# Modulation sums as column groups inside the value projection, squares of two layer norms added on VectorE

## The reference, cut to what matters

```python
cs = jax.nn.silu(c)
for i in range(2):
    mod = cs @ ada_w[i] + ada_b[i]                 # 1024 -> 3072
    shift, scale, gate = jnp.split(mod, 3, axis=-1)
    h = x * (1.0 + scale) + shift
    y = moba_branch(h, ...) if i == 0 else gdn_branch(h, ...)
    x = layer_norm(ALPHA * x + gate * y, ln_g[i], ln_b[i])
```

## Time and profile before

| | before |
|---|---|
| median of three runs | 837.98 us |
| profiled execution: span from first to last instruction | 836.7 us |
| TensorE matmul busy | 818.6 us, 98% |
| TensorE weight load busy | 764.5 us, 91% |
| VectorE busy | 613.2 us, 73% |
| ScalarE busy | 488.0 us, 58% |
| GpSimd busy | 67.8 us, 8% |
| bytes moved | 153.85 MB, mean 184 GB/s |

### The profile page before, as it was taken

The page is one execution under the profiler, slowest core; times in us unless marked ns, Lnnn a source line. Parts: engine busy times, 40 slices in busy tenths (PEclk is TensorE's granted clock), DMA queues, the critical chain, the costliest instruction groups (busy, mean ns, idle before and its releaser), DMA issues.

```text
span 836.7 us, 17639 instructions
## 1 busy us (share of the span) xinstructions
PE 818.6 (98%) x6596; PEld 764.5 (91%) x6596; DVE 613.2 (73%) x1052; ACT 488.0 (58%) x901; POOL 67.8 (8%) x71
## 2 busy tenths in 40 slices
PE   6999999999999999999999999999999999999997
PEld 3899988999998998989898888999999999999885
DVE  4497876768889666977877779664777996888543
ACT  3444476567699754584665457566556554555444
POOL 1000002400001002224100011000002120000000
PEclk9999999999999999999999999999999999999999
DMA  9999963804452221445543426433445444554521
GB/s 373 389 361 389 362 260 140 348 14 139 172 191 103 102 103 52 157 146 192 212 159 143 152 84 219 152 136 141 178 177 201 167 186 156 196 174 177 201 101 50
DMA packets 22012, 153.85 MB, mean 184 GB/s; under 512 B 2496, under 2 KB 2752, under 8 KB 3904
## 3 DMA queue, kind: packets, MB, share of 16 engines
q1 hardware_dynamic: 20592, 145.69, 47.7%
q0 software_dynamic: 1360, 7.34, 2.4%
HBM read 151.97 MB, written 1.05 MB: 183 GB/s over the span
## 4 chain that ended last, share of the span: by engine, by line
PE 83%; DVE 6%; DMA 5%; ACT 3%; issue 2%; SPq 0%; DVEq 0%; ACTq 0%
PE ps L403 41%; PE ps L1277 7%; PE ps L506 7%; PE ps L476 4%; DVE w_lo L1970 3%; PE ps L437 2%; PE ps L843 2%; DMA raw<-in_mixed 2%; PE ps L446 1%; PE ps L468 1%; ACT w_hi L1317 1%; DMA raw<-in_moba_first 1%; DMA proj<-in_ada_first 1%; PE ps L580 1%; PE ps L603 1%
## 5 line engine op out<-in xcount | busy, mean ns | idle before, releaser
L1970 DVE TENSOR_TENSOR w_lo<-raw,w_hi 128x1024 fp32r<-128x1024 f32 x230 | 285.8, 1247 | 95.6 <-ACT w_hi L1317 94.2
L1317 ACT CAST w_hi<-raw 128x1024 fp32r<-128x1024 f32 (+1 forms) x230 | 239.8, 1050 | 165.1 <-PE ps L403 63.1
L403 PE MATMUL ps<-in_hi,w_hi 128*128 128x256 f32 x1120 | 160.7, 286 | 0.5 <-DVE w_lo L1970 0.5
L403 PE MATMUL ps<-in_lo,w_hi 128*128 128x256 f32 x1120 | 157.2, 283 | 0.0
L403 PE MATMUL ps<-in_hi,w_lo 128*128 128x256 f32 x1120 | 157.1, 283 | 0.0
L403 PEld LDWEIGHTS ps<-in_hi,w_hi 128*128 128x128 f32 x1120 | 144.3, 191 | 4.9 <-issue 3.7
L403 PEld LDWEIGHTS ps<-in_hi,w_lo 128*128 128x128 f32 x1120 | 144.5, 192 | 0.0
L403 PEld LDWEIGHTS ps<-in_lo,w_hi 128*128 128x128 f32 x1120 | 144.3, 192 | 0.0
L2235 DVE SCALAR_TENSOR_TENSOR proj<-work,params,proj 128x256 f32 (+1 forms) x72 | 35.7, 496 | 8.0 <-ACT proj L1537 1.9
L2047 DVE SCALAR_TENSOR_TENSOR work<-raw,cs,work 128x1024 f32 x24 | 30.8, 1284 | 4.8 <-DVE w_lo L1970 1.6
L1277 PE MATMUL ps<-w_hi,in_hi 128*128 128x512 f32 x88 | 34.2, 389 | 0.0
(11 more groups left out here) (444 smaller groups left out, 1350.6 us busy)
## 6 DMA issues: line engine op xcount, KB each, us to landing
raw<-in_mixed SPq DMA_DIRECT2D x24, 1024.0 KB, 7.1
raw<-in_ffn_up SPq DMA_DIRECT2D x22, 1024.0 KB, 4.8
raw<-in_gdn_in SPq DMA_DIRECT2D x16, 1024.0 KB, 4.8
raw<-in_w_in SPq DMA_DIRECT2D x16, 1024.0 KB, 4.8
raw<-in_merge SPq DMA_DIRECT2D x12, 1024.0 KB, 4.7
raw<-in_ffn_down SPq DMA_DIRECT2D x11, 1024.0 KB, 4.8
raw<-in_branch SPq DMA_DIRECT2D x6, 1024.0 KB, 4.7
raw<-in_moba_out SPq DMA_DIRECT2D x4, 1024.0 KB, 7.2
```

Of the source, the lines that this page charges most:

```text
L403: mm = pe.matmul(half(u if bank is None else bank, 0), w[:, u, k * P:(k + 1) * P], a[:, base + k, :], start=(n == 0 and k == 0), stop=(n = ...
L1317: act.copy(w_hi[:, u, :], src).then_inc(hi_done, 1)
L1970: dve.tensor_tensor(w_lo[:, u, :], src, w_hi[:, u, :].bitcast(F32), ALU.subtract).then_inc(lo_done, 1)
```

## The change

Three edits. **First**, `add_partitions` sums all three chunks at once, behind `moba_values(0)` and a wait for all 24 blocks: 12 matmuls, ones as weights of 32 columns, the accumulator streaming in quarters of 256 columns to four groups of 32 output partitions. ScalarE copies the rows out, six transposes between `moba_values(1)` and `moba_values(2)` turn them, and VectorE adds the biases there; ln0 has no modulation left. **Second**, the late products of chunk 5 run in one go before the squares of ln0, one column group per part, are copied by ScalarE and turned by two transposes behind the squares; the matmuls of L819 are gone, and `keep_warm` issues three instead of four. **Third**, in ln0 and ln1 VectorE adds the eight square tiles into one (`add_squares`), and TensorE sums that one; in ln0 one low part moves from ahead of `centre` to behind the additions, in ln1 the sum moves into unit 2 of `mem_kv`, ahead of its last eight matmuls.

```diff
@@ -252,7 +252,8 @@
     late_in = [area(0, PAIR * D, of=kv_flat)] + [area(PAIR * D * n, PAIR * D, of=flat_proj) for n in range(3)]
-    late_rows = vnat_flat
+    late_rows = area(0, S, of=vnat_flat)
+    mod_rows = area(3072, 3 * S)
     gain = area(4096, D)
@@ -281,6 +282,12 @@
         return t.rearrange("p a b -> p (a b)")
+    mod_banks = flat(ps[:, 6:8, :])[:, 0:3 * S]
+    def turned_columns(v):
+        return v.rearrange("p (x q r) -> p q x r", x=2, q=4)[:, :, :, 0]
@@ -393,10 +400,12 @@
     def _(pe):
-        def unit(u, tag=None, base=0, bank=None):
+        def unit(u, tag=None, base=0, bank=None, before_last=None):
             for n, (w, a) in enumerate(((w_hi, in_hi), (w_hi, in_lo), (w_lo, in_hi))):
+                if n == 2 and before_last:
+                    before_last()
                 for k in range(UNIT):
@@ -414,14 +423,12 @@
-        def project_short(name, tag, base=0, between={}, first=0, count=None):
+        def project_short(name, tag, base=0, within={}, first=0, count=None):
                 pe.wait_ge(taken, FIRST[name] + n + 1)
-                unit(n % GROUP, tag if n == 0 else None, base)
-                if n in between:
-                    between[n]()
+                unit(n % GROUP, tag if n == 0 else None, base, before_last=within.get(n))
@@ -491,12 +498,10 @@
-        def sum_tiles(out, src, ready, name, tiles=KT):
-            for k in range(tiles):
-                pe.wait_ge(*after(ready, k + 1))
-                mm = pe.matmul(out, ones, src[:, k, :], start=(k == 0), stop=(k == tiles - 1))
-            mm.then_inc(sem(name), 1)
+        def sum_squares(tag):
+            pe.wait_ge(sem(f"{tag}_added"), 1)
+            pe.matmul(half(5, 0), ones, sq_of[tag][:, 0, :], start=True, stop=True).then_inc(sem(f"{tag}_sumsq"), 1)
@@ -643,13 +648,20 @@
-        def add_partitions(chunks, name):
-            for c in chunks:
-                for n in range(KT):
-                    mm = pe.matmul(ps[:, 7, c * KT + n:c * KT + n + 1], acc[:, c, n * P:(n + 1) * P], ones[:, 0:1],
-                                   start=True, stop=True)
-            mm.then_inc(sem(name), 1)
+        def add_partitions():
+            for c in range(3):
+                for q in range(4):
+                    mm = pe.matmul(half(6 + c // 2, c % 2)[32 * q:32 * q + 32, :], ones[:, 0:32],
+                                   acc[:, c, q * S:(q + 1) * S], start=True, stop=True)
+            mm.then_inc(sem("mod_rows"), 1)
+        def turn_rows():
+            pe.wait_ge(sem("mod_copied"), 1)
+            for n in range(6):
+                mm = pe.transpose(mod_banks[:, n * P:(n + 1) * P], mod_rows[:, n * P:(n + 1) * P], ident)
+            mm.then_inc(sem("mod_columns"), 1)
@@ -723,9 +735,11 @@
         pe.wait_ge(*after("consts_in", 16))
-        pe.wait_ge(lo_done, MIXED + 16)
-        add_partitions(range(0, 1), "mod_gate")
-        for n in range(1, GROUP):
+        pe.wait_ge(lo_done, PLAIN)
+        add_partitions()
+        moba_values(1)
+        turn_rows()
+        for n in range(2, GROUP):
             moba_values(n)
@@ -788,36 +802,22 @@
-        def sum_squares(tag):
-            sum_tiles(half(5, 0), sq_of[tag], f"{tag}_sq", f"{tag}_sumsq")
         sum_total(half(4, 0), "ln0", lambda k: (x_t, (taken, all_taken("moba_out", k + 1))), "ln0_sum")
-        def late_products(p):
-            pe.wait_ge(sem("late_in"), 16 * 4)
-            for k in range(KT):
-                q = 32 * (k % 4)
-                mm = pe.matmul(ps[q:q + 32, (6, 4)[p // 2], (p % 2) * S:(p % 2 + 1) * S], cs_wide[:, k, :],
-                               late_in[p][:, k * S:(k + 1) * S], start=(k < 4), stop=(k >= 4))
-            if p % 2:
-                mm.then_inc(sem("late_products"), 1)
-        late_products(0)
-        late_products(1)
-        add_partitions(range(1, 2), "mod_rest")
+        pe.wait_ge(sem("late_in"), 16 * 4)
+        for k in range(KT):
+            for q in range(4):
+                mm = pe.matmul(half(6, 0)[32 * q:32 * q + 32, :], cs_wide[:, k, :], late_in[q][:, k * S:(k + 1) * S],
+                               start=(k == 0), stop=(k == KT - 1))
+        mm.then_inc(sem("late_products"), 1)
         sum_squares("ln0")
-        add_partitions(range(2, 3), "mod_rest")
-        pe.wait_ge(*after("ln0_centred", KT))
-        late_products(2)
-        late_products(3)
-        keep_warm(4, 3)
+        pe.wait_ge(sem("late_copied"), 1)
+        for x in range(2):
+            mm = pe.transpose(half(7, 0)[:, x * P:(x + 1) * P], late_rows[:, x * P:(x + 1) * P], ident)
+        mm.then_inc(sem("late_columns"), 1)
+        keep_warm(3, 3)
         first_units("gdn_in", "in2")
-        pe.wait_ge(*after("late_copied", 2))
-        for n in range(KT):
-            mm = pe.matmul(ps[:, 5, n:n + 1], late_rows[:, n * P:(n + 1) * P], one, start=True, stop=True)
-        mm.then_inc(sem("late_columns"), 1)
         pe.wait_ge(sem("gate_w_lo"), 2)
@@ -1115,7 +1115,7 @@
         memory_pass(2).then_inc(unit_done, 1)
-        project_short("mem_kv", None, base=MEM_IN, between={1: lambda: sum_squares("ln1")}, first=1, count=4)
+        project_short("mem_kv", None, base=MEM_IN, within={2: lambda: sum_squares("ln1")}, first=1, count=4)
         for n in range(4, 8):
@@ -1504,7 +1504,10 @@
-        for n in range(28, 32):
+        high("moba_in", 28)
+        act.wait_ge(sem("mod_rows"), 1)
+        act.copy(mod_rows, mod_banks).then_inc(sem("mod_copied"), 1)
+        for n in range(29, 32):
             high("moba_in", n)
@@ -1516,6 +1519,8 @@
         squares("ln0", x_t, "ln0_centred")
+        act.wait_ge(sem("late_products"), 1)
+        act.copy(late_rows, half(6, 0)).then_inc(sem("late_copied"), 1)
         root("ln0", LN_EPS)
@@ -1526,10 +1531,6 @@
                 act.copy(in_hi[:, k - 1, :], h_t[:, k - 1, :]).then_inc(sem("in2_hi"), 1)
-        for n, bank in enumerate((6, 4)):
-            act.wait_ge(*after("late_products", n + 1))
-            act.copy(late_rows[:, n * 512:(n + 1) * 512], ps[:, bank, :]).then_inc(sem("late_copied"), 1)
         def evac_conv(i, u):
@@ -2012,14 +2013,6 @@
-        def modulation(at, chunks, column, one_plus=None):
-            link(dve.tensor_tensor(flat_mod[:, KT * at:KT * (at + chunks)], ps[:, 7, column:column + KT * chunks],
-                                   param("ada_b", KT * at, KT * chunks), ALU.add))
-            if one_plus is not None:
-                scale = flat_mod[:, one_plus * KT:one_plus * KT + KT]
-                link(dve.tensor_scalar(scale, scale, 1.0, None, ALU.add))
         pair_of = lambda v: v.rearrange("p (a b) -> p a b", a=2)
@@ -2117,12 +2110,20 @@
-        dve.wait_ge(*after("mod_gate", 1))
-        modulation(2, 1, 0)
+        low("moba_in", 28)
+        dve.wait_ge(sem("mod_columns"), 1)
+        for c in range(2, 5):
+            by_pair = lambda v: v.rearrange("p (q x) -> p q x", q=4)
+            ins = dve.tensor_tensor(by_pair(flat_mod[:, KT * c:KT * c + KT]), turned_columns(mod_banks[:, (c - 2) * S:(c - 1) * S]),
+                                    by_pair(param("ada_b", KT * c, KT)), ALU.add)
+        link(ins)
         dve.sem_inc(sem("mod_read"), 1)
-        for n in range(28, 31):
-            low("moba_in", n)
+        low("moba_in", 29)
+        link(dve.tensor_scalar(mod[:, 1, 8:16], mod[:, 1, 8:16], 1.0, None, ALU.add))
+        link(dve.tensor_tensor(ln_bias[:, 0, :], param("ln_b", 0, KT), mod[:, 1, 8:16], ALU.mult))
+        link(dve.tensor_tensor(ln_bias[:, 0, :], ln_bias[:, 0, :], mod[:, 1, 0:8], ALU.add))
+        link(dve.tensor_scalar(ln_bias[:, 1, :], param("ln_b", 0, KT), ALPHA, None, ALU.mult))
+        low("moba_in", 30)
         dve.wait_ge(*after("consts_in", 16))
@@ -2185,6 +2186,16 @@
+        def add_squares(tag):
+            v = sq_of[tag]
+            dve.wait_ge(*after(f"{tag}_sq", 4))
+            dve.tensor_tensor(v[:, 0:2, :], v[:, 0:2, :], v[:, 2:4, :], ALU.add)
+            dve.wait_ge(*after(f"{tag}_sq", KT))
+            link(dve.tensor_tensor(v[:, 4:6, :], v[:, 4:6, :], v[:, 6:8, :], ALU.add))
+            link(dve.tensor_tensor(v[:, 0:2, :], v[:, 0:2, :], v[:, 4:6, :], ALU.add))
+            dve.tensor_tensor(v[:, 0, :], v[:, 0, :], v[:, 1, :], ALU.add).then_inc(sem(f"{tag}_added"), 1)
         def invert(tag):
@@ -2202,13 +2213,11 @@
             residual("moba_out", n, mod[:, 0, 16 + n:17 + n])
-            low("moba_out", n + GROUP)
+            if n < KT - 1:
+                low("moba_out", n + GROUP)
         centre("ln0")
-        dve.wait_ge(*after("mod_rest", 2))
-        modulation(3, 2, KT, one_plus=4)
-        link(dve.tensor_tensor(ln_bias[:, 0, :], param("ln_b", 0, KT), mod[:, 1, 8:16], ALU.mult))
-        link(dve.tensor_tensor(ln_bias[:, 0, :], ln_bias[:, 0, :], mod[:, 1, 0:8], ALU.add))
-        link(dve.tensor_scalar(ln_bias[:, 1, :], param("ln_b", 0, KT), ALPHA, None, ALU.mult))
+        add_squares("ln0")
+        low("moba_out", KT - 1 + GROUP)
         invert("ln0")
```

(4 more changed lines are left out.)

## The result

The changed kernel takes 841.71 us (median of 7 runs, 837.06 to 844.26), the kernel before on the same chip 838.41 (7 runs). The ratio is 1.0033, 95% interval 1.0019 to 1.0048: slower by 0.33%, 2.8 us; the two medians differ by 3.3. 841.3 was forecast. The median is nearly the forecast's; the trace shows that this isn't because every term was.

The account below looks back on a forecast made before the run. TensorE, almost never idle in a hand-written order, was taken to bound the kernel. Terms: wait +6.8, clock +2.3, ln0 -3.4, columns 0, ln1 -2.4, together +3.3 on 837.98, giving 841.3 us; range 838.4 to 843.6.

Parts of the forecast that it names:

- The added wait, +6.8: Value projection: TensorE idles 6.5 us for the last `ada_w` block, plus sums 1.6, transposes 0.7, less 2.0 removed.
- rival (b): Value projection: last block added x earlier than 107.75, gap shrinks by x, clock holds; faster from x = 2.7; chance 0.09.
- a hole under 4 us: Sign against the prediction: TensorE's hole behind the first value piece, forecast at 6.5 us, measures under 4 us.
- an attention less than 6 us later: Sign against the prediction: the attention starts less than 6 us later than in the kernel before.
- The clock, +2.3: Behind the value projection's hole: TensorE's clock falls to its lower level, costing 2.3 us; bounds nothing and 2.3.
- ln0, -3.4: Layer norm 0: scaling starts 3.0 us earlier, and the shorter hold before the first unit gives 0.4 more.
- Rival (d): Layer norm 0: its gaps bring the clock down there too, another 2.3 us, total 843.6; chance 0.08.
- The columns, 0: Behind gdn_in's first units: 1.84 us of records go, but VectorE's chain ends last, so gain 0; bounds 0 and -1.8.
- Rival (c): Behind gdn_in's first units: the columns' 1.8 us are kept as gain, total 839.5; chance 0.08.
- ln1, -2.4: Layer norm 1: sixteen square-sum records become two, -2.8 us, less 0.2 of waiting and 0.2 lost.
- hangs on ScalarE's squares, which don't move: Step in the ln1 term: GpSimd's running sum for the next norm, ending at 380.25, stays put; 0.2 us lost.
- Rival (a), the clock holds: Value projection: the clock stays up through the gap, so the change costs +1.0, total 839.0; chance 0.15.

Follow-up runs that it names:

- after: The changed kernel itself, in its first profiled execution, the fastest of seven: 837.06 us (median of the seven 841.71 us, ratio 1.0033).
- after_again: The changed kernel, unaltered, run once more for a second profile: 841.51 us, ratio 1.0032 to the kernel before.
- gap_warm: The changed kernel with 8 matmuls on constants, result unread, ahead of TensorE's wait for all blocks: 841.32 us, ratio 1.0033 to the kernel before.
- gap_full: The changed kernel with 13 matmuls on constants in the hole ahead of the sums by column groups: 839.54 us, ratio 1.0015 to the kernel before.
- hole: Kernel before with column-group sums behind the third value piece, ln1 additions, and a TensorE wait for the gate activation before gdn_in's later groups: 840.43 us.
- sums_only: The kernel before with only the first edit (sums by column groups); squares, late products and columns unchanged: 843.29 us, ratio 1.0056.
- filler_late: The changed kernel, sums behind the third value piece, plus four unread matmuls where chunk 5's column products stood: 834.23 us, ratio 0.9956 to the kernel before.

## Why the prediction was right, and where it wasn't

**The added wait, +6.8: right mechanism, wrong as a fixed size.** The hole is there, ended by VectorE's last addition, and nothing behind it gives it back. But 6.5 was read from one execution, and the last block's end differs between executions by 4 us: 104.65 and 106.01 in the changed kernel, 104.81 to 108.69 in the others, 107.75 in before. Before, TensorE doesn't wait for that block and no run shows it; in the four traces with the sums in this place (`after`, `after_again`, `gap_warm`, `gap_full`) the time follows the start of the sums, and the clock where it fell, within 0.5 us. The changed kernel's seven runs spread over 7.2 us, the seven of before beside them over 2.4 (later sets: 3.5 of 7 runs, 4.1 of 24). The prediction took the block's pace for that of the weights arriving. That is half of it: in `after_again` VectorE's last five blocks, each with its low part, follow each other every 2.6 to 2.8 us, with pauses of 0.35 at most, so at the end VectorE's own work sets the pace. What differs stands before: ScalarE's longest wait for a load, at 73 to 79 us, is 3.42 in the fastest execution, 4.55 in `after_again`, 4.84 in before. That the loads make the spread is argued from these waits; no run held them fixed. A last block earlier by x was rival (b), and the fastest execution is it: x = 3.1, the clock held. The forecast gives 841.3 - 2.3 - 3.1 = 835.9 for it and it took 837.06. The execution nearest to the median that has a trace (`after_again`, 841.66) had 5.2. The prediction named a hole under 4 us and an attention less than 6 us later as signs against it: both were so in the fastest execution, neither in the next (5.19; 119.35 is 7.9 later).

**The clock, +2.3: right that it falls, too small.** The median run's mean clock is 0.995, and the fall cost 2.76 in `after_again`, above the 2.3 that the prediction held for the upper bound. It didn't at 3.85 us and did at 4.32, 4.71 and 5.19. The start of the kernel was the right place to look: the granted clock reads 0.50 behind the hole, and 1.00 at the start, where records take twice their time all the same. The Trainium skill ("TensorE: Matmul & The Clock Gate", the section on why this matters) has a gap between bursts bring the clock down. `hole` and `after_again` agree; in the gap of 3.85 us it did not happen.

**ln0, -3.4: right, -3.45, though the additions don't earn it.** The centre, the additions, the root and the hold of `keep_warm` came as written. But `sums_only` has all but 0.1 of it without the additions on VectorE. Two things were late before: the squares' sum, because the sums of chunk 3 stood ahead of it on TensorE, and the scaling, because VectorE waited for the modulation and made five small operations behind it; 1.7 us each, and both leave with the sums. The prediction followed the new chain rightly, centre, additions, root, but it is no gain of the additions: the scaling starts 8.35 us behind the total in the whole change (164.89 to 173.24) and 8.05 without them. Rival (d) is refuted: the two gaps of 1.6 and 1.5 us leave the clock at its upper level.

**The columns, 0: right**, -0.13 by the trace and nothing in `filler_late`. Rival (c) falls.

**ln1, -2.4: mis-sized.** -1.87, and -1.9 alone. The step that failed is "hangs on ScalarE's squares, which don't move": the running sum began 0.4 earlier, but GpSimd's five additions grew from 7.49 to 8.27 us beside VectorE's bunched low parts.

**Rival (a), the clock holds:** true in one of the first seven runs of the changed kernel, and made true in nearly all by `gap_full`: 839.54, where the rival said 839.0.

The sum with what was measured, for a run like the profiled one of `after_again`: hole 5.2, sums and transposes 0.6 (4.48 less the 3.85 of the fastest execution), clock 2.8, ln0 -3.45, columns -0.1, ln1 -1.9: +3.1 against a measured +2.8 (by the ratio) to +3.3 (by the medians), and +3.1 between the two spans. This execution also reaches the first value piece 0.7 earlier than the one of before and loses 0.6 in stretches that have no term, so the last tenths of that match are chance. The forecast of +3.3 had 1.3 too much in the hole, 0.3 too little in the sums and transposes, 0.5 too little in the clock and 0.5 too much gain in ln1. The mechanisms of the hole, the clock and ln0 were there, but that these errors cancel to within 0.5 us is luck.

## What to carry to other kernels

A cheaper form of a sum that needs *all* of its inputs moves the wait from the early inputs to the last one. Place it behind the independent work that was behind it: here that alone turned +2.7 us into -4.4, by the ratios. The length of an instruction could be read from one execution here, but not the moment at which work that hangs on loads is done: take several, above all where nothing waits for it yet. And where a gain appears beside two edits, run one without the other before naming its cause.

## What the hardware showed beyond expectation

- With the same loads, VectorE was done with the last block of `ada_w` at 104.65 to 108.69 us in fourteen profiled executions.
- TensorE's clock, by the granted column: up through idle gaps of 1.5, 1.6, 2.1 and 3.85 us, down behind 4.32, 4.71 and 5.19; what it cost was 1.3 to 2.8 us. At the start of the kernel 12 records took 4.60 us and the next 12 took 2.20, and the column read 1.00 in both the earlier trace rows.
- GpSimd's addition of 128x256 took 0.74 us at its shortest and 1.65 beside VectorE's low parts; a low part of 128x1024 took 1.2 without GpSimd and 1.6 beside it.
- 24 records in four column groups, 32 columns of weights each, took 1.50 us, the last one's tail with it: some 0.06 each, where full-width records of 256 columns (8 in 1.12 us, tail included) follow each other every 0.12.
